# Eight expert weight tiles ahead instead of four, and the token rows written later

## The chip, the cores and the metric

The kernel runs on one core of one Trainium2 chip. The metric is the device time of one execution in microseconds (us). The engines are TensorE (PE; its weight loads are listed as PEld), VectorE (DVE), ScalarE (ACT), GpSimd (POOL) and SyncE (SP), which issues most of the DMA transfers. POOL issues the rest, among them the indirect ones, whose rows are picked by an index tile.

## The reference

256 tokens of width 1024 pass through two blocks, all in float32. The first has an HGRN/RG-LRU mixer, a convolutional feed-forward, an attention and a second feed-forward. The second has latent attention, a SwiGLU feed-forward, an S5 mixer, and at the end a mixture of experts. Only this last part is touched:

```
logits = t @ w_router                       # 256 tokens, 8 experts
top_vals, top_idx = lax.top_k(logits, 2)
gates = softmax(top_vals)
for e in range(8):                          # d_ff of an expert: 3584
    he  = (silu(t @ w_gate[e]) * (t @ w_up[e])) @ w_down[e]
    out = out + combine[:, e] * he
```

The reference runs every token through every expert and weighs by `combine`, which is zero but for a token's two experts. The kernel computes only the tokens that chose an expert.

## The kernel before

**Tiles of weights.** An expert has 28 tiles of 128 hidden columns, all eight have 224. A tile is 1.5 MB in float32: 1 MB for gate and up (`UP`), 0.5 MB for down (`DOWN`). They stream from memory once.

**Places in SBUF.** All weights ahead of the experts go through four slots of 3 MB, in turn, as 57 units (`LOADED`). The last four units are the second of the S5 input projection (slot 1) and the three of the S5 gated projection (`s5_glu`: slots 2, 3, 0). PE adds to `slot_free` when it is through with a unit (L1617): with `s5_glu` this is after output tiles 5, 11 and 15. The experts' ring of four tiles (`ups`, `downs`, L430 to L432) has three up parts in slot 1, and the fourth with the four down parts in slot 2. Slots 3 and 0 (`lone`, L434) hold the token rows: `hrow` (normalized tokens to be scattered), `xl` (rows of the next expert, read back) and `returned` (results read back).

**SP's order.** After the last unit SP waits for slots 1 and 2, loads tiles 0 to 3 into the ring (L490 to L496), and waits until PE has done the up part of tile 0 (L498). From then on it reloads the up part of a place as soon as PE's up part of the tile there is done (`up_ready`, L502), and the down part when PE's down part is (`moe_free`, L504).

**Gathering.** If no expert has over 96 tokens (`CAP`), which holds here, PE takes the `experts_gathered` path. It gathers the tokens of experts 0 and 1 from SBUF by two sets of matmuls (`gather`, L1772). The tokens of the later experts go through memory. DVE writes `hrow` (L2683). POOL waits for it and for the row numbers (`rows`, L549), scatters the rows into `rows_in` by four indirect DMAs (L551), and loads the rows of expert 2 into `xl` (`load`, L546). Expert 2's rows are needed by `turn_rows` at the end of expert 0. Rows of further experts follow, one load an expert, and each expert's result is stored (L561). At the last expert four indirect DMAs read results back (L564).

**PE's order.** `up(j)` is 64 weight loads and 64 matmuls as the trace counts them, `down(j)` 32 and 32. `four(e, i)` (L1846) is four tiles: up of tile j+1, then down of tile j. The program has it written out four times: in a loop of seven inside the loop over experts 0 to 5, in a loop of seven for expert 6, in a loop of six for expert 7, and once for the last four tiles. Between experts come `turn_rows`, `open_sums`, `turn_sums`. ACT (silu, L960) and DVE (`hidden`, L2647) work on each tile in between.

If an expert has over 96 tokens, a dense path runs in place of this (`experts_dense`); it did not run in the profiled execution.

Of the kernel before, what the change touches and what calls it, by code (L numbers as in the profile page):

```python
# [168 lines left out]
def build_program(nc, a):  # L169

    ctx = ExitStack()
    with ctx:
# [226 lines left out]
        gain_row = yT[:, 0:4].rearrange("p a n -> p (a n)")  # L399
        xg = part(12, 3).rearrange("p (a n) -> p a n", a=KD)  # L400
        first_picks = [part(i)[:, 0:2 * CAP].rearrange("p (g n) -> p g n", g=2) for i in (22, 23)]
        ye = part(18, 4)[0:CAP]
        weighted = part(17)[:, 0:2 * CAP].rearrange("p (g n) -> p g n", g=2)
        place = part(23)[0:CAP]
        ysum = part(26, 3).rearrange("p (a n) -> p a n", a=KD)
        posm = part(24)[:, 0:2 * 8].rearrange("p (g n) -> p g n", g=2)
# [22 lines left out]

        ring_slots = [(len(LOADED) - SLOTS + k) % SLOTS for k in range(2)]  # L430
        ups = [slots[ring_slots[h // 3]][:, h % 3 * UP:(h % 3 + 1) * UP] for h in range(RING)]
        downs = [slots[ring_slots[1]][:, UP + h * DOWN:UP + (h + 1) * DOWN] for h in range(RING)]  # L432

        lone = [slots[(len(LOADED) - SLOTS + k) % SLOTS] for k in (2, 3)]  # L434
        hrow = lone[0][:, 0:2 * D].rearrange("p (g d) -> p g d", g=2)
        xl = lone[0][0:CAP, 2 * D:3 * D]
        returned = lone[1][:, 0:4 * D].rearrange("p (n d) -> p n d", n=4)
        where = part(25)[:, 16:64].rearrange("p (n c) -> p n c", c=8)
# [7 lines left out]
        def _(sp):  # L446
# [8 lines left out]
            for name in STREAM:  # L455
                sizes, u0, w = phase_units(name), UNIT0[name], a["w_" + name]

                def load(u, unit, name=name, sizes=sizes, w=w, u0=u0):

                    sp.wait_ge(slot_free, unit + u0 + 1)  # L460
                    sp.dma_start(slots[(u0 + u) % SLOTS][:, 0:sizes[u]],
                                 w[bass.ds(unit, 1), :, 0:sizes[u]].rearrange("o p n -> p (o n)")
                                 ).then_inc(slot_loaded[(u0 + u) % SLOTS], 16)

                fours = len(sizes) // SLOTS if name in FFN and name != "ffn2" else 0
                if fours:
                    with sp.Fori(0, fours) as i:
                        for u in range(SLOTS):
                            load(u, i * SLOTS + u)
                for u in range(fours * SLOTS, len(sizes)):  # L470
                    if name == "even_in" and u == 0:
                        continue
                    load(u, u)
                    if name == "ffn2" and u == SLOTS - 1:
                        sp.wait_ge(x_ready, 6 * KD)
                        sp.dma_start(cT, a["s5_cT"]).then_inc(s5_loaded, 16)
                        sp.dma_start(bexp, a["s5_b"]).then_inc(s5_loaded, 16)
                    if name == "even_in" and u == 1:
                        for dst, small in ((rgw[:, :, :, :], "rgw"), (wf[:, :, :], "wf"),
                                           (wr[:, :, :], "wr"), (pos_i[:, :], "positions")):  # L480
                            sp.dma_start(dst, a[small]).then_inc(late_loaded, 16)
            def load_up(h, unit):
                sp.dma_start(ups[h], a["w_moe"][bass.ds(unit, 1), :, 0:UP].rearrange(
                                 "o p n -> p (o n)")).then_inc(moe_up_loaded[h], 16)
# [4 lines left out]

            for h in range(RING):  # L490
                for s in ring_slots[0:1 if h < 3 else 2]:
                    sp.wait_ge(slot_free, SLOTS + max(n for n in range(len(LOADED))
                                                      if n % SLOTS == s) + 1)
                load_up(h, h)
            for h in range(RING):
                load_down(h, h)  # L496
            last = EXPERTS * FE_TILES // RING - 1
            sp.wait_ge(up_ready, 2 * FT0["moe"] + 2)  # L498
            load_up(0, RING)
            with sp.Fori(1, last) as i:  # L500
                for h in range(RING):
                    sp.wait_ge(up_ready, i * (2 * RING) + (2 * (FT0["moe"] + h - RING) + 4))  # L502
                    load_up((h + 1) % RING, i * RING + (h + 1))
                    sp.wait_ge(moe_free, i * RING + h + 1)  # L504
                    load_down(h, i * RING + h)
# [15 lines left out]
        def _(pool):  # L521
# [26 lines left out]
            pool.wait_ge(mo["scattered"], ZEROED)  # L548
            pool.wait_ge(mo["rows"], 3)  # L549
            for n in range(4):  # L550
                pool.indirect_dma_start(  # L551
                    out=rows_in, out_offset=bass.IndirectOffsetOnAxis(ap=slot_row[:, n:n + 1], axis=0),
                    in_=hrow[:, n // 2], in_offset=None).then_inc(mo["scattered"], 16)
# [505 lines left out]
        def _(pe):  # L1059
# [643 lines left out]

            def up_weights(f, rounds):

                pe.wait_ge(moe_up_loaded[f % RING], rounds * 16 + 16 * (f // RING + 1))
                return ups[f % RING]

            def down_weights(f, rounds):

                pe.wait_ge(moe_down_loaded[f % RING], rounds * 16 + 16 * (f // RING + 1))
                return downs[f % RING]

            def experts_dense():
# [20 lines left out]
                for b in range(4):  # L1735
                    pe.matmul(ps[:, b, 0:1], ident, mask[:, 0:1], start=True, stop=False,
                              skip_group_check=True)
                with pe.Fori(0, EXPERTS) as e:
                    def up(f):
                        w = up_weights(f, e * (FE_TILES // RING))  # L1740
                        for k in range(2):
# [6 lines left out]
                    def down(f):  # L1748
                        w = down_weights(f, e * (FE_TILES // RING))
                        pe.wait_ge(hid_ready, e * FE_TILES + (FT0["moe"] + f + 1))  # L1750
# [6 lines left out]
                    for f in range(FE_TILES):  # L1757
                        if f + 1 < FE_TILES:
                            up(f + 1)
                        down(f)  # L1760
                pe.wait_ge(moe_free, RING + EXPERTS * FE_TILES)
                pe.sem_inc(acc_ready, KD)
# [7 lines left out]
            def experts_gathered():  # L1770
# [49 lines left out]
                def up(j, loads, inputs=None):  # L1820

                    pe.wait_ge(moe_up_loaded[j], loads)
                    for k in range(2):
                        for c in range(KD):
                            if inputs is not None and k == 0 and c % 4 == 0:
                                pe.wait_ge(mo["xready"], inputs + c // 4)
                            for s in range(0, P, STRIP):
                                o = (k * KD + c) * P + s
                                m = pe.matmul(gate_up(j, k)[s:s + STRIP],  # L1829
                                              ups[j][:, o:o + STRIP], xg[:, c], start=c == 0,  # L1830
                                              stop=c == KD - 1, skip_group_check=True)
                        m.then_inc(up_ready, 1)

                def down(j, loads, hids):

                    pe.wait_ge(moe_down_loaded[j], loads)
                    pe.wait_ge(hid_ready, hids)
                    for d in range(KD):
                        for s in range(0, P, STRIP):
                            o = d * P + s  # L1840
                            m = pe.matmul(y_sum(d)[s:s + STRIP], downs[j][:, o:o + STRIP],  # L1841
                                          hid[j][:, 0:CAP], start=False, stop=False,
                                          skip_group_check=True)
                    m.then_inc(moe_free, 1)

                def four(e, i, last=False):  # L1846

                    def at(scale, plus):
                        return e * (GROUPS * scale) + i * scale + plus

                    for j in range(RING):
                        if j < RING - 1:
                            up(j + 1, at(16, 16))
                        elif not last:
                            up(0, at(16, 32), at(2, 3))
                        down(j, at(16, 16), at(RING, FT0["moe"] + j + 1))

# [9 lines left out]
                gather(1)  # L1867
                up(0, 16, 1)
                open_sums(None)
                with pe.Fori(0, EXPERTS - 2) as e:  # L1870
                    with pe.Fori(0, GROUPS) as i:
# [70 lines left out]
        def _(dve):  # L1942
# [685 lines left out]
            def experts_gathered():  # L2628
# [52 lines left out]
                dve.wait_ge(mo["htaken"], 4)  # L2681
                for g in range(2):
                    dve.tensor_scalar(hrow[:, g], vtok[:, g], col[:, 2 + g:3 + g], None, ALU.mult  # L2683
                                      ).then_inc(mo["rows"], 1)
                for e in range(EXPERTS):
                    for f in range(FE_TILES):
# [4 lines left out]
                        if f == FE_TILES - 1 and e < EXPERTS - 1:  # L2691
                            dve.wait_ge(up_ready, 2 * (e * FE_TILES + FT0["moe"] + f) + 2)
                            take_input(e + 1)
                        hidden(e, f)
                        if e and f == 0:
                            take_turned(e - 1)
# [14 lines left out]
            def experts():  # L2711
                with dve.If(dve.value_load(crowded[0:1, 0:1], min_val=0, max_val=1) == 1):
                    dve.sem_inc(mo["rows"], 2)
                    dve.sem_inc(mo["yeready"], 2 * EXPERTS)
                    for g in range(2):
                        dve.tensor_scalar(mixd[g], ident, col[:, 2 + g:3 + g], None, ALU.mult
# [207 lines left out]
```

## Time and profile before

| | |
|---|---|
| median of 3 runs (lowest, highest) | 2221.22 us (2219.17, 2222.02) |
| profiled execution, span | 2221.2 us |
| profiled execution, own time | 2221.22 us, the same as its span |
| PE busy, DVE busy, ACT busy, POOL busy | 97%, 38%, 21%, 1% |
| the experts' first matmul on weights | 1291.91 us |
| weights of the experts | 224 tiles, 1 MB and 0.5 MB each |

All times of rows are counted from the start of the span. A busy PE is not PE at its peak, since the ends of matmuls are modelled; the rate is better read from the starts of like groups. PEld rows give where the weight loads stood still. "<-issue" at a row's end is idle time for which the profile shows no releaser. In the list of DMA queues q1 is SP's, q0 is POOL's, and q8 carries instructions.

### The profile page before, as it was taken

To read this page: it belongs to the slowest core of one execution; us is meant where nothing else is said; L and a number is where in the kernel's file an instruction comes from. 1 tells how busy PE (TensorE), PEld (TensorE's weight loads), DVE (VectorE), ACT (ScalarE), POOL (GpSimd) and SP (SyncE) were. 2 spreads that over 40 slices of the span, in tenths; PEclk is the share of its full clock that TensorE was granted. 3 is DMA by queue.
4 is the path that set the end of the run, shared out by engine and by line. 5 is a ranking of instruction groups with operands and counts; after the bars stand their busy time and mean duration, and the time that the engine had idled before them with its cause. 6 is when DMAs were issued, how large, how long until landed. Compare 5 with 4: busy or idle time off the path is not lost.

```text
span 2221.2 us, 67406 instructions
## 1 busy us (share of the span) xinstructions
PE 2161.3 (97%) x30418; PEld 2003.8 (90%) x30418; DVE 839.7 (38%) x2085; ACT 467.8 (21%) x1074; POOL 24.9 (1%) x43
## 2 busy tenths in 40 slices
PE   9999999999999999999987999999999999999998
PEld 8889999857999986999966889999999999999998
DVE  4257666224766636567769120101010101010102
ACT  3432112123211234110043121111111111111112
POOL 1000000000000000000000000000000000000000
PEclk9999999999999999999999999999999999999999
DMA  9242344232144322444322169999999999999996
GB/s 393 91 171 86 152 161 190 95 132 111 68 164 171 138 90 100 159 164 171 133 115 96 58 258 400 392 394 392 396 392 397 389 398 389 398 382 399 390 409 249
DMA packets 78400, 535.04 MB, mean 241 GB/s; under 512 B 8913, under 2 KB 9042, under 8 KB 41938
## 3 DMA queue, kind: packets, MB, share of 16 engines
q1 hardware_dynamic: 74450, 519.82, 59.6%
q0 software_dynamic: 3840, 13.63, 1.7%
q8 instruction: 83, 1.36, 0.3%
q14 instruction: 27, 0.22, 0.0%
HBM read 523.20 MB, written 10.22 MB: 240 GB/s over the span
## 4 chain that ended last, share of the span: by engine, by line
PE 69%; DVE 3%; ACT 1%; issue 1%; DVEq 0%; ACTq 0%
PE ps L1829 27%; PE ps L1841 13%; PE ps L1202 11%; PE ps L1244 7%; PE ps L1119 4%; PE ps L1611 2%; PE ps L1594 1%; DVE scr L2501 0%; PE ps L1793 0%; PE ps L1802 0%; PE ps L1135 0%; PE ps L1481 0%; PE ps L1467 0%; PE ps L1548 0%; PE ps L1443 0%
## 5 line engine op out<-in xcount | busy, mean ns | idle before, releaser
L1829 PE MATMUL ps<-scr,slot 128*64 128x96 f32 x14336 | 640.2, 246 | 3.2 <-issue 3.2
L1829 PEld LDWEIGHTS ps<-scr,slot 128*64 128x64 f32 x14336 | 613.0, 137 | 6.7 <-issue 6.6
L2650 DVE TENSOR_TENSOR scr<-scr,ps 128x96 f32<-128x96 f32 x224 | 56.8, 254 | 767.0 <-ACT scr L960 767.0
L1841 PE MATMUL ps<-scr,slot 128*64 128x96 f32 x7168 | 341.6, 246 | 1.3 <-issue 1.3
L1841 PEld LDWEIGHTS ps<-scr,slot 128*64 128x64 f32 x7168 | 317.0, 137 | 1.5 <-issue 1.5
L1244 PE MATMUL ps<-scr,slot 128*128 128x256 f32 x1056 | 237.6, 379 | 1.6 <-DVE scr L2321 1.6
L960 ACT ACTIVATE scr<-ps 128x96 f32<-128x96 f32 x224 | 56.3, 251 | 786.4 <-PE ps L1829 786.4
L1244 PEld LDWEIGHTS ps<-scr,slot 128*128 128x128 f32 x1056 | 196.2, 190 | 26.4 <-DVE scr L2321 2.0
L1202 PE MATMUL ps<-vtok,slot 128*128 128x128 f32 x1056 | 139.5, 275 | 0.0
L1202 PEld LDWEIGHTS ps<-vtok,slot 128*128 128x128 f32 x1056 | 128.8, 192 | 0.2
L1202 PE MATMUL ps<-vtok,proj 128*128 128x128 f32 x1056 | 128.7, 275 | 0.0
L1202 PEld LDWEIGHTS ps<-vtok,proj 128*128 128x128 f32 x1056 | 123.2, 192 | 0.0
L1202 PEld LDWEIGHTS ps<-hT,slot 128*128 128x128 f32 x960 | 116.2, 192 | 2.8
L1202 PE MATMUL ps<-hT,slot 128*128 128x128 f32 x960 | 116.9, 275 | 0.0
L1119 PE MATMUL ps<-hT,slot 128*128 128x256 f32 x416 | 94.1, 384 | 0.6 <-PE ps L1119 0.6
L2247 DVE TENSOR_TENSOR proj<-slot 128x512 f32<-128x512 f32 x132 | 91.1, 690 | 6.2 <-ACT mixT L724 2.9
L817 ACT ACTIVATE sq<-ps 128x128 f32<-128x128 f32 x66 | 18.3, 278 | 351.4 <-PE ps L1202 351.4
L1119 PEld LDWEIGHTS ps<-hT,slot 128*128 128x128 f32 x416 | 79.1, 192 | 13.7 <-issue 3.1
L1298 PE MATMUL ps<-hT,slot 128*128 128x256 f32 x384 | 88.3, 389 | 2.0 <-DMA slot<-in_w_even_in 1.7
L1298 PEld LDWEIGHTS ps<-hT,slot 128*128 128x128 f32 x384 | 74.6, 196 | 13.9 <-DMA slot<-in_w_even_in 1.9
L1119 PE MATMUL ps<-mixT,slot 128*128 128x256 f32 x384 | 84.6, 381 | 1.3 <-PE ps L1119 0.9
L1119 PEld LDWEIGHTS ps<-mixT,slot 128*128 128x128 f32 x384 | 72.4, 190 | 13.1 <-issue 3.0
(412 smaller groups left out, 2044.8 us busy)
## 6 DMA issues: line engine op xcount, KB each, us to landing
slot<-in_w_moe SPq DMA_DIRECT2D x224, 1024.0 KB, 7.0
slot<-in_w_moe SPq DMA_DIRECT2D x224, 512.0 KB, 6.9
slot<-in_w_ffn SPq DMA_DIRECT2D x33, 3072.0 KB, 10.7
slot<-in_w_even_in SPq DMA_DIRECT2D x3, 3072.0 KB, 27.5
slot<-in_w_odd_qk SPq DMA_DIRECT2D x2, 3072.0 KB, 10.5
slot<-in_w_s_glu SPq DMA_DIRECT2D x2, 3072.0 KB, 11.8
slot<-in_w_odd_v SPq DMA_DIRECT2D x2, 2048.0 KB, 8.1
slot<-in_w_even_in SPq DMA_DIRECT2D x2, 1536.0 KB, 10.6
```

What stands on the lines that cost most here:

```text
L817: act.activation(mid(k, 0), product(k, P1), ACT.Copy).then_inc(first_copied, 1)
L960: act.activation(gbuf[j][:, 0:CAP], gate_up(j, 0), ACT.Silu).then_inc(gate_act, 1)
L1119: m = pe.matmul(ps[:, bank0 + n % ring, 0:T], w[:, o:o + P], src[:, c], start=c == 0, stop=c == k - 1, skip_group_check=True)
L1202: m = pe.matmul(product(k, n), weights[:, c * P:(c + 1) * P], x[:, c], start=first and c == 0, stop=c == 3, skip_group_check=True)
L1244: m = pe.matmul(acc(d), w[:, o:o + P], hid2[u % 2][:, half], start=u == half == 0 and d % 2 == 0, stop=last, skip_group_check=True)
L1298: m = pe.matmul(even_tile(i), project.w[:, o:o + P], hT[:, c], start=c == 0, stop=c == KD - 1, skip_group_check=True)
L1594: m = pe.matmul(ps[k:k + 32, q % 2, a:b], w[:, r, q, k:k + 32], x[:, j, 0:n], start=False, stop=i == 3, skip_group_check=True)
L1611: m = pe.matmul(glu_tile(i), w[:, o:o + P], hT[:, c], start=c == 0, stop=c == KD - 1, skip_group_check=True)
L1829: m = pe.matmul(gate_up(j, k)[s:s + STRIP], ups[j][:, o:o + STRIP], xg[:, c], start=c == 0, stop=c == KD - 1, skip_group_check=True)
L1841: m = pe.matmul(y_sum(d)[s:s + STRIP], downs[j][:, o:o + STRIP], hid[j][:, 0:CAP], start=False, stop=False, skip_group_check=True)
L2247: dve.tensor_tensor(dst, a, b, ALU.subtract).then_inc(combined, 1)
L2650: dve.tensor_tensor(hid[f % 4][:, 0:CAP], gbuf[f % 4][:, 0:CAP], gate_up(f, 1), ALU.mult).then_inc(hid_ready, 1)
```

## The change

The ring of four moves from slots 1 and 2 to slots 3 and 0. Tiles 0 to 3 of the first expert get places of their own in slots 1 and 2 (`lead_ups`, `lead_downs`), with the same layout; the ring begins with tile 4. `hrow`, `xl` and `returned` move from slots 3 and 0 to slots 1 and 2, over the lead tiles, so DVE and POOL now wait until the lead tiles are used up (`moe_free` 8: four down parts done; its count starts at four). DVE writes the two halves of `hrow` after `hidden` of tiles 4 and 5 of expert 0. SP loads the lead tiles, then the ring as slots 3 and 0 come free, and waits for the up part of tile 4 before it reloads. PE writes the first four tiles out on their own, then has a loop of six for the rest of expert 0, then the loop over experts 1 to 5. The dense path, the narrowing of two tiles to their used columns, and a count added to `dve_own` in the dense path go with it.

```diff
-        ring_slots = [(len(LOADED) - SLOTS + k) % SLOTS for k in range(2)]
-        lone = [slots[(len(LOADED) - SLOTS + k) % SLOTS] for k in (2, 3)]
-        hrow = lone[0][:, 0:2 * D].rearrange("p (g d) -> p g d", g=2)
+        lead_slots, ring_slots = ([(len(LOADED) - SLOTS + k) % SLOTS for k in some]
+                                  for some in ((0, 1), (2, 3)))
+        lead_loaded = [_n[k] + 16 * n for k, n in zip(lead_slots, (3, 1 + RING))]
+        lead_ups, lead_downs = up_places(lead_slots), down_places(lead_slots)
+        ups, downs = up_places(ring_slots), down_places(ring_slots)
+        lead = [slots[k] for k in lead_slots]
+        hrow = lead[0][:, 0:2 * D].rearrange("p (g d) -> p g d", g=2)
...
             for h in range(RING):
+                for s in lead_slots[0:1 if h < 3 else 2]:
+                    sp.wait_ge(slot_free, left(s))
+                sp.dma_start(lead_ups[h], a["w_moe"][h, :, 0:UP]
+                             ).then_inc(slot_loaded[lead_slots[h // 3]], 16)
+            for h in range(RING):
+                sp.dma_start(lead_downs[h], a["w_moe"][h, :, UP:UP + DOWN]
+                             ).then_inc(slot_loaded[lead_slots[1]], 16)
+            for h in range(RING):
                 for s in ring_slots[0:1 if h < 3 else 2]:
-                load_up(h, h)
+                    sp.wait_ge(slot_free, left(s))
+                load_up(h, RING + h)
             for h in range(RING):
-                load_down(h, h)
+                load_down(h, RING + h)
-            sp.wait_ge(up_ready, 2 * FT0["moe"] + 2)
-            load_up(0, RING)
-            with sp.Fori(1, last) as i:
+            sp.wait_ge(up_ready, 2 * (FT0["moe"] + RING) + 2)
+            load_up(0, 2 * RING)
+            with sp.Fori(2, last) as i:
...
             pool.wait_ge(mo["rows"], 3)
+            pool.wait_ge(moe_free, RING + RING)
...
-                up(0, 16, 1)
+                up(0, None, 1)
                 open_sums(None)
-                with pe.Fori(0, EXPERTS - 2) as e:
+                four(0, 0, first=True)
+                with pe.Fori(1, GROUPS) as i:
+                    four(0, i)
+                turn_rows(16)
+                open_sums(2)
+                turn_sums(2)
+                with pe.Fori(1, EXPERTS - 2) as e:
...
-                for g in range(2):
-                    dve.tensor_scalar(hrow[:, g], vtok[:, g], col[:, 2 + g:3 + g], None, ALU.mult
-                                      ).then_inc(mo["rows"], 1)
...
                         hidden(e, f)
+                        if e == 0 and f in (RING, RING + 1):
+                            g = f - RING
+                            dve.wait_ge(moe_free, RING + RING)
+                            dve.tensor_scalar(hrow[:, g], vtok[:, g], col[:, 2 + g:3 + g], None,
+                                              ALU.mult).then_inc(mo["rows"], 1)
```

## Rows read from the trace of the kernel before

**Rows 1.** The page: busy time of PE; DMA share in 40 slices.

```profile
PE 2161.3 (97%) x30418; PEld 2003.8 (90%) x30418; DVE 839.7 (38%) x2085; ACT 467.8 (21%) x1074; POOL 24.9 (1%) x43
DMA  9242344232144322444322169999999999999996
```

**Rows 2.** Waits of PE and PEld, 1290 to 2221 us: total us, times, longest.

```profile
PE ps L1829 <- issue: 3.2, 10, 0.5
...
PEld ps L1829 <- issue: 6.6, 17, 1.2
```

**Rows 3.** Busy time by stretch: PE, PEld, DVE, ACT, POOL, clock, DMA, GB/s.

```profile
1320.00:1405.00 85.00, 85.00 (x2066) 85.00 (x2064) 5.34 (x21) 11.69 (x26) 0.00 (x0) 1.00 1.01 401
```

**Rows 4.** Timeline of PEld from the experts' start: start us, us, instructions.

```profile
1295.19 1.59 PEld L1829 LDWEIGHTS ps<-scr,slot 128*64 128x64 f32 x37
...
1299.83 0.44 PEld L1829 LDWEIGHTS ps<-scr,slot 128*64 128x64 f32 x9 [1.14 <-issue]
1300.15 1.44 PEld L1841 LDWEIGHTS ps<-scr,slot 128*64 128x64 f32 x32
1301.47 2.76 PEld L1829 LDWEIGHTS ps<-scr,slot 128*64 128x64 f32 x64
1304.11 1.44 PEld L1841 LDWEIGHTS ps<-scr,slot 128*64 128x64 f32 x32
...
1312.03 1.37 PEld L1841 LDWEIGHTS ps<-scr,slot 128*64 128x64 f32 x31
...
1315.47 2.82 PEld L1829 LDWEIGHTS ps<-scr,slot 128*64 128x64 f32 x63 [0.45 <-issue]
```

**Rows 5.** Timeline of POOL's DMA issues.

```profile
1294.19 1.04 POOL L551 DMA_INDIRECT rows_in<-slot,idx  x1 [1164.66 <-DVE slot L2683]
...
1298.09 0.96 POOL L551 DMA_INDIRECT rows_in<-slot,idx  x1 [0.30 <-issue]
1309.50 0.58 POOL L546 DMA_DIRECT2D slot<-rows_in  x1 [10.45 <-DMA rows_in<-slot,idx]
1412.83 0.53 POOL L546 DMA_DIRECT2D slot<-rows_in  x1 [102.75 <-PE ps L1793]
...
2102.80 1.01 POOL L564 DMA_INDIRECT slot<-rows_out,idx  x1 [4.51 <-DMA rows_out<-scr]
```

**Rows 6.** Timeline of PEld in the first passes for experts 6 and 7.

```profile
1986.71 2.70 PEld L1829 LDWEIGHTS ps<-scr,slot 128*64 128x64 f32 x64
...
1998.59 2.70 PEld L1829 LDWEIGHTS ps<-scr,slot 128*64 128x64 f32 x64
...
2104.35 0.30 PEld L1829 LDWEIGHTS ps<-scr,slot 128*64 128x64 f32 x5
...
2110.04 0.14 PEld L1841 LDWEIGHTS ps<-scr,slot 128*64 128x64 f32 x1
```

**Rows 7.** DMA queue q8, 1291 to 1317 us: packets, MB, share.

```profile
q8 instruction: 3, 0.05, 0.8%
```

**Rows 8.** The same queue, 1983 to 2004 us.

```profile
q8 instruction: 3, 0.05, 0.9%
```

**Rows 9.** SP's queue, 1301 to 1304 us.

```profile
q1 hardware_dynamic: 1, 0.00, 0.0%
```

**Rows 10.** L483, up parts from 1291 us on: issue to landing.

```profile
DMA to landing us min/median/max: 5.9/7.0/10.9
```

**Rows 11.** Timeline of SP's DMA issues around the experts' start.

```profile
1207.78 33.65 SPq L483 DMA_DIRECT2D slot<-in_w_moe  x4
...
1294.79 6.21 SPq L483 DMA_DIRECT2D slot<-in_w_moe  x2
```

**Rows 12.** Timeline of PEld behind `s5_glu` output tiles 11 and 15.

```profile
1264.26 0.20 PEld L1677 LDWEIGHTS ps<-cst,xT 128*128 128x128 f32 x2 [0.68 <-issue]
...
1279.75 0.20 PEld L1677 LDWEIGHTS ps<-cst,xT 128*128 128x128 f32 x2 [0.52 <-issue]
```

**Rows 13.** Timeline of DVE ahead of tile 0's hidden product.

```profile
1291.94 1.41 DVE L2683 TENSOR_SCALAR slot<-vtok,col 128x1024 f32<-128x1024 f32 x2
```

More of the change, by code:

```diff
@@ L399, in build_program @@
         gain_row = yT[:, 0:4].rearrange("p a n -> p (a n)")
-        xg = part(12, 3).rearrange("p (a n) -> p a n", a=KD)
+        xg = part(12, 3)[:, 0:KD * CAP].rearrange("p (a n) -> p a n", a=KD)
         first_picks = [part(i)[:, 0:2 * CAP].rearrange("p (g n) -> p g n", g=2) for i in (22, 23)]
@@ L404, in build_program @@
         place = part(23)[0:CAP]
-        ysum = part(26, 3).rearrange("p (a n) -> p a n", a=KD)
+        ysum = part(26, 3)[:, 0:KD * CAP].rearrange("p (a n) -> p a n", a=KD)
         posm = part(24)[:, 0:2 * 8].rearrange("p (g n) -> p g n", g=2)
@@ L428, in build_program, with up_places, down_places @@
         mix0 = {"even_out": 0, "odd_out": KD, "mla_o": 2 * KD}
-        ring_slots = [(len(LOADED) - SLOTS + k) % SLOTS for k in range(2)]
-        ups = [slots[ring_slots[h // 3]][:, h % 3 * UP:(h % 3 + 1) * UP] for h in range(RING)]
-        downs = [slots[ring_slots[1]][:, UP + h * DOWN:UP + (h + 1) * DOWN] for h in range(RING)]
-        lone = [slots[(len(LOADED) - SLOTS + k) % SLOTS] for k in (2, 3)]
-        hrow = lone[0][:, 0:2 * D].rearrange("p (g d) -> p g d", g=2)
-        xl = lone[0][0:CAP, 2 * D:3 * D]
-        returned = lone[1][:, 0:4 * D].rearrange("p (n d) -> p n d", n=4)
+        lead_slots, ring_slots = ([(len(LOADED) - SLOTS + k) % SLOTS for k in some]
+                                  for some in ((0, 1), (2, 3)))
+        def up_places(two):
+            return [slots[two[h // 3]][:, h % 3 * UP:(h % 3 + 1) * UP] for h in range(RING)]
+        def down_places(two):
+            return [slots[two[1]][:, UP + h * DOWN:UP + (h + 1) * DOWN] for h in range(RING)]
+        lead_loaded = [_n[k] + 16 * n for k, n in zip(lead_slots, (3, 1 + RING))]
[3 more added lines that the diff above has]
+        hrow = lead[0][:, 0:2 * D].rearrange("p (g d) -> p g d", g=2)
+        xl = lead[0][0:CAP, 2 * D:3 * D]
+        returned = lead[1][:, 0:4 * D].rearrange("p (n d) -> p n d", n=4)
         where = part(25)[:, 16:64].rearrange("p (n c) -> p n c", c=8)
@@ L481, in _, with left @@
                             sp.dma_start(dst, a[small]).then_inc(late_loaded, 16)
+            def left(s):
+                return SLOTS + max(n for n in range(len(LOADED)) if n % SLOTS == s) + 1
             def load_up(h, unit):
@@ L490, in _ @@
             for h in range(RING):
+                for s in lead_slots[0:1 if h < 3 else 2]:
[6 more added lines that the diff above has]
+            for h in range(RING):
                 for s in ring_slots[0:1 if h < 3 else 2]:
-                    sp.wait_ge(slot_free, SLOTS + max(n for n in range(len(LOADED))
-                                                      if n % SLOTS == s) + 1)
-                load_up(h, h)
+                    sp.wait_ge(slot_free, left(s))
+                load_up(h, RING + h)
             for h in range(RING):
-                load_down(h, h)
+                load_down(h, RING + h)
             last = EXPERTS * FE_TILES // RING - 1
-            sp.wait_ge(up_ready, 2 * FT0["moe"] + 2)
-            load_up(0, RING)
-            with sp.Fori(1, last) as i:
+            sp.wait_ge(up_ready, 2 * (FT0["moe"] + RING) + 2)
+            load_up(0, 2 * RING)
+            with sp.Fori(2, last) as i:
                 for h in range(RING):
@@ L1702, in router, with up_weights, down_weights @@
                           skip_group_check=True).then_inc(mo["pos"], 1)
-            def up_weights(f, rounds):
-                pe.wait_ge(moe_up_loaded[f % RING], rounds * 16 + 16 * (f // RING + 1))
-                return ups[f % RING]
-            def down_weights(f, rounds):
-                pe.wait_ge(moe_down_loaded[f % RING], rounds * 16 + 16 * (f // RING + 1))
+            def up_weights(e, f, first):
+                if first and f < RING:
+                    pe.wait_ge(slot_loaded[lead_slots[f // 3]], lead_loaded[f // 3])
+                    return lead_ups[f]
+                pe.wait_ge(moe_up_loaded[f % RING], e * (16 * GROUPS) + 16 * (f // RING))
+                return ups[f % RING]
+            def down_weights(e, f, first):
+                if first and f < RING:
+                    pe.wait_ge(slot_loaded[lead_slots[1]], lead_loaded[1])
+                    return lead_downs[f]
+                pe.wait_ge(moe_down_loaded[f % RING], e * (16 * GROUPS) + 16 * (f // RING))
                 return downs[f % RING]
@@ L1737, in experts_dense, with expert @@
                               skip_group_check=True)
-                with pe.Fori(0, EXPERTS) as e:
+                def expert(e, first):
                     def up(f):
-                        w = up_weights(f, e * (FE_TILES // RING))
+                        w = up_weights(e, f, first)
                         for k in range(2):
@@ L1748, in down @@
                     def down(f):
-                        w = down_weights(f, e * (FE_TILES // RING))
+                        w = down_weights(e, f, first)
                         pe.wait_ge(hid_ready, e * FE_TILES + (FT0["moe"] + f + 1))
@@ L1760, in experts_dense @@
                         down(f)
+                expert(0, True)
+                with pe.Fori(1, EXPERTS) as e:
+                    expert(e, False)
                 pe.wait_ge(moe_free, RING + EXPERTS * FE_TILES)
@@ L1820, in up @@
                 def up(j, loads, inputs=None):
-                    pe.wait_ge(moe_up_loaded[j], loads)
+                    if loads is None:
+                        pe.wait_ge(slot_loaded[lead_slots[j // 3]], lead_loaded[j // 3])
+                    else:
+                        pe.wait_ge(moe_up_loaded[j], loads)
+                    w = lead_ups[j] if loads is None else ups[j]
                     for k in range(2):
@@ L1829, in up @@
                                 m = pe.matmul(gate_up(j, k)[s:s + STRIP],
-                                              ups[j][:, o:o + STRIP], xg[:, c], start=c == 0,
+                                              w[:, o:o + STRIP], xg[:, c], start=c == 0,
                                               stop=c == KD - 1, skip_group_check=True)
@@ L1834, in down @@
                 def down(j, loads, hids):
-                    pe.wait_ge(moe_down_loaded[j], loads)
+                    if loads is None:
+                        pe.wait_ge(slot_loaded[lead_slots[1]], lead_loaded[1])
+                    else:
+                        pe.wait_ge(moe_down_loaded[j], loads)
+                    w = lead_downs[j] if loads is None else downs[j]
                     pe.wait_ge(hid_ready, hids)
@@ L1840, in down @@
                             o = d * P + s
-                            m = pe.matmul(y_sum(d)[s:s + STRIP], downs[j][:, o:o + STRIP],
+                            m = pe.matmul(y_sum(d)[s:s + STRIP], w[:, o:o + STRIP],
                                           hid[j][:, 0:CAP], start=False, stop=False,
@@ L1844, in down, with four @@
                     m.then_inc(moe_free, 1)
-                def four(e, i, last=False):
+                def four(e, i, last=False, first=False):
                     def at(scale, plus):
                         return e * (GROUPS * scale) + i * scale + plus
+                    here = None if first else at(16, 0)
                     for j in range(RING):
                         if j < RING - 1:
-                            up(j + 1, at(16, 16))
+                            up(j + 1, here)
                         elif not last:
-                            up(0, at(16, 32), at(2, 3))
-                        down(j, at(16, 16), at(RING, FT0["moe"] + j + 1))
+                            up(0, at(16, 16), at(2, 3))
+                        down(j, here, at(RING, FT0["moe"] + j + 1))
                 def open_sums(copies):
@@ L2714, in experts @@
                     dve.sem_inc(mo["yeready"], 2 * EXPERTS)
+                    dve.sem_inc(dve_own, 4)
                     for g in range(2):
```

## The prediction

> **What bounds the kernel now.** I read the page first, then the waits of PE, the stretches, the timelines of PE's weight loads, of POOL and of SP, and last the DMA queues. The page has PE busy for 97% of the span and the DMA engines at nine tenths from about 1290 us on [rows 1], so both could bound the experts. The stretches leave that open too: from 1320 to 1405 us PE shows no gap and DMA a share of 1.01 at 401 GB/s [rows 3]. Three rows decide it. No wait of PE behind 1290 us has a DMA as its releaser; what there is stands as "issue" [rows 2]. A tile takes 3.96 us, from one group of down loads at 1300.15 to the next at 1304.11, of which the up part is 2.64 and the down part 1.32 [rows 4]. A place of the ring is used again four tiles later, so its up part may take 15.84 - 2.64 = 13.2 us from issue to landing; the median is 7.0 and the longest 10.9 [rows 10]. PE sets the pace, weights come in time, and the 224 tiles cost 224 x 3.96 = 887 us whatever is loaded ahead.
>
> So the change can win only where PE stands still at the experts' beginning, and that is in two places. Up of tile 1 begins at 1295.19, and its down loads follow at 1300.15, 4.96 us later where 2.64 is usual: 2.32 us lost. A down part begins at 1312.03 and the next up part at 1315.47, 3.44 us for 1.32: 2.12 us lost [rows 4]. Together 4.4 us. Neither is a wait for weights: both stops fall inside a part, between loads from one tile that is already there. The queue that carries instructions moved three packets between 1291 and 1317 us [rows 7], while PE goes through its loop for the first time, so I read both stops as PE running out of instructions. That reading has a condition. Three packets were moved from 1983 to 2004 us too, as PE first went through expert 6's loop [rows 8], and the ups there keep their pace: from 1986.71 to 1998.59 are 11.88 us for three tiles, 3.96 each [rows 6]. What differs is POOL. Its four scatters are issued from 1294.19 to 1298.09, around the first stop, the load of expert 2's rows at 1309.50, just ahead of the second, and the four gathers of the results from 2102.80 [rows 5], around a third stop: an up part that begins at 2104.35 and reaches its down loads at 2110.04, 5.69 us for 2.64, 3.05 lost [rows 6]. So: new code costs 2 to 3 us where POOL's scatters, gathers or row loads are under way, and nothing beside weights and one plain store.
>
> **The change part by part.**
>
> *Loads ahead.* The lead tiles take the same places at the same times as tiles 0 to 3 now, from 1207.78 us on [rows 11]. New are the ring's first four tiles: 3 MB after `s5_glu` tile 11, at about 1264.3, and 3 MB after tile 15, at about 1279.8 [rows 12]. At 400 GB/s [rows 3] each takes 7.9 us (an estimate), so both have landed at about 1290, with DMA empty there before. The start of PE at 1295.19 hangs on the router's small steps, which touch no DMA: cost 0. If that cover fails it is one packet of code fetched beside 3 MB of weights, from 0 [rows 8] to 3.05 us [rows 6].
>
> *SP.* Its first reload now waits for the up part of tile 4: 1295.19 + 3 x 3.96 + 2.64 = 1309.7 us, against 1294.79 now [rows 11]. Behind that wait stand only later reloads, each with its 13.2 us as before. The stream ends no earlier and no later for PE: 0.
>
> *First four tiles.* They become straight code. From 1295.19 to 1311.0 us neither weights nor POOL move anything. I take the stop of 2.32 us as gone; the ends are 0 and 2.32 kept.
>
> *Token rows.* DVE loses two writes of 1.41 us together ahead of tile 0's hidden product [rows 13]; nobody waited for DVE there, so 0. They come back after tiles 4 and 5. The first waits for four down parts, at 1311.0; what is queued behind it is `hidden` of tile 5, not due before up of tile 5 ends at 1313.7, and the write takes half of 1.41. The second follows that product. Both are covered: 0. POOL's scatter then starts at about 1315 us (21 us later), and expert 2's rows are loaded 1309.50 - 1294.19 = 15.3 us behind it [rows 5], at about 1330; they are needed near 1410, so 0 by themselves.
>
> *Loop of six.* A new piece of code, entered at 1311.0 and through its first pass at 1326.9. The scatter falls into the middle of it, 4 us after entry; the gathers of expert 7 fell 6 us into a like pass and cost 3.05. I take the mean of the two measured scatter or gather stops, (2.32 + 3.05) / 2 = 2.7 us; the ends are 0 and 2.32 + 2.12 = 4.4. The load at 1330 comes when the pass is over, so I count no second stop.
>
> *Loop of experts 1 to 5.* One more piece that PE enters new, near 1412, as POOL loads rows at 1412.83 [rows 5] and stores a result. Expert 6's pass had the store alone and no stop [rows 6]. I take 0; the ends are 0 and 4.4.
>
> *Late weights.* The longest landing, 10.9 us, was reached with PE stopped for 4.4 us meanwhile, and with SP's queue getting nothing through from 1301 to 1304 [rows 9]. Without any stop it could be 10.9 + 4.4 = 15.3, 2.1 us over the 13.2. A stop of 2.7 in the same place gives that time back, so the two don't add: 0 beside it.
>
> Sum: -2.32 - 2.12 + 2.7 = -1.7 us. The profiled execution's own time is its span, 2221.2, which is also the median; so 2219.5.
>
> **A rule against it.** The two stops and a like pass without one are what the rows show [rows 4, 6]. The Trainium skill's page "Runtime: NRT & Kernel Launch", section "Instruction fetch mechanics", says that fetching runs ahead in sequence only, and that a taken branch whose target is outside a small window of pages stalls until the target is fetched. By that rule each new loop would pay at its back jump; the second stop does stand at the end of a first pass, but later passes of the same loop keep 3.96 a tile, which speaks against it as a general price. What it would make of this kernel is the third rival below.
>
> **The rivals.**
>
> 1. *No stop left.* The quiet four tiles also bring the code of the loop in time, and the scatter meets none that is new: -4.4, 2216.8. For: expert 6's pass. Against: all three passes with POOL's transfers had a stop.
> 2. *More code, more stops* (the other side). POOL's plain loads and stores are enough to hold up new code. Then both new loops have two stops: 2.7 + 2.12 in the loop of six and 2.32 + 2.12 in the next, 9.2 in place of 4.4, so +4.8, 2226.0. It decides from the entry into the loop of experts 1 to 5: a stop there makes it. For: the second stop came beside a plain load. Against: expert 6 with a store.
> 3. *The back jump.* Each new loop's first end costs 2.12: 2.7 + 2 x 2.12 = 6.9 against 4.4, so +2.5, 2223.7. For: where the second stop stands. Against: expert 7's loop shows none at its end.
> 4. *The stream is the bound after all.* Four tiles more ahead would then be worth 4 x 3.96 = 15.8 us: 2205.4. For: a DMA share of 1.01. Against: landings of 7.0 us for 13.2, and no wait of PE for a DMA. Here the change would do what its loads suggest; in all other cases they are simply not needed.
> 5. *The weights come late or the early loads disturb the router*: the stop at the first four or at 1290 stays or is replaced, +2.1 to +3.05 on the forecast, 2221.6 to 2222.6.
>
> **How the numbers follow.** Forecast 0.38, rival 1 0.17, rival 2 0.16, rival 3 0.12, rival 4 0.05, rival 5 0.12. A measurement of this kernel can tell about 0.2%, 4.4 us, from no change. Rival 4 and a good half of rival 1 are faster than that: 0.17. Most of rival 2 and a little of rivals 3 and 5 are slower: 0.17. The rest, 0.66, is the same within 0.2%. The range leaves out rival 4 and a few cases where stops add up: 2214 to 2227.5. The forecast's own range is 2217 to 2222.
>
> **What would show it.** Right: SP's loads at about 1264 and 1280 us; the tiles from 1295 to 1311 at 3.96 each; scatters from 1315; one stop of 2 to 3 us between 1315 and 1327; the entry near 1412 at full pace; no wait of PE for a DMA. Wrong: a stop before 1311 with nothing moving (then POOL is not the cause); a stop behind 1412; a wait for weights; a later start than 1295; or a tile that takes other than 3.96 us.

## The result: 3 us slower, and the profile after

The changed kernel takes 2222.43 us (median of 20 runs, 2218.90 to 2228.82), the kernel before 2219.51 us in 20 runs beside it (2217.65 to 2222.97). The ratio is 1.0014, 95% interval 1.0008 to 1.0021, so the change costs about 3.1 us (1.8 to 4.7). I had forecast 1.7 us less. The profiled execution of the changed kernel took 2219.58 us and its span is 2217.5 us: what lies around a span is about 2 us (1.8 to 2.4 in the other profiles below that list both). The profile of before that I worked from, with a span of 2221.2, therefore belongs to an execution of some 2223.3 us (an estimate), almost 4 above the median. My step "the profiled execution's own time is its span, 2221.2, which is also the median" was wrong, and so is the line of the table of times above that says the same. Two executions, of 4534 us (before, beside e5 to e8) and 5309 us (e8), took more than twice the usual time and are left out of all medians and ratios.

The page of the changed kernel: the queue that carries instructions moved 89 packets, where it moved 83 before (the line by itself), six more for the code that is written out.

```profile
span 2217.5 us, 67375 instructions
...
q8 instruction: 89, 1.46, 0.3%
```

```profile
q8 instruction: 83, 1.36, 0.3%
```

PEld's timeline from the experts' start, the counterpart of [rows 4]:

```profile
1294.97 2.67 PEld L1866 LDWEIGHTS ps<-scr,slot 128*64 128x64 f32 x64
...
1310.78 2.70 PEld L1866 LDWEIGHTS ps<-scr,slot 128*64 128x64 f32 x64
1313.42 1.38 PEld L1882 LDWEIGHTS ps<-scr,slot 128*64 128x64 f32 x32
1314.74 1.38 PEld L1866 LDWEIGHTS ps<-scr,slot 128*64 128x64 f32 x32
1316.50 1.35 PEld L1866 LDWEIGHTS ps<-scr,slot 128*64 128x64 f32 x32 [0.38 <-issue]
1317.80 1.38 PEld L1882 LDWEIGHTS ps<-scr,slot 128*64 128x64 f32 x32
1319.12 2.70 PEld L1866 LDWEIGHTS ps<-scr,slot 128*64 128x64 f32 x64
1323.37 1.36 PEld L1882 LDWEIGHTS ps<-scr,slot 128*64 128x64 f32 x32 [1.55 <-issue]
...
1329.81 2.91 PEld L1866 LDWEIGHTS ps<-scr,slot 128*64 128x64 f32 x64 [0.32 <-issue]
```

The four written-out tiles run from 1294.97 to 1310.78: 15.8 us, their full pace. The first pass through the loop of six runs from there to 1329.81: 19.0 us for 15.84, so 3.2 lost. Read in the same way, the first pass of before lost 4.4 [rows 4].

SP's and POOL's issues, the counterparts of [rows 11] and [rows 5]:

```profile
1262.23 16.02 SPq L497 DMA_DIRECT2D slot<-in_w_moe  x4
1278.29 2.35 SPq L501 DMA_DIRECT2D slot<-in_w_moe  x4
1309.75 4.47 SPq L497 DMA_DIRECT2D slot<-in_w_moe  x2
```

```profile
1315.75 1.04 POOL L573 DMA_INDIRECT rows_in<-slot,idx  x1 [1186.23 <-PE ps L1882]
...
1319.65 0.96 POOL L573 DMA_INDIRECT rows_in<-slot,idx  x1 [0.30 <-issue]
1334.07 0.58 POOL L567 DMA_DIRECT2D slot<-rows_in  x1 [13.46 <-DMA rows_in<-slot,idx]
```

The up parts of the ring from issue to landing, for [rows 10]; a place allows 13.2 us:

```profile
DMA to landing us min/median/max: 4.9/7.0/12.3
```

And stretches, with the columns of [rows 3]: the gathers, the four lead tiles, and behind the scatter.

```profile
1284.00:1292.00 8.00, 7.29 (x136) 7.30 (x138) 4.51 (x22) 2.27 (x3) 0.00 (x0) 0.79 0.41 167
1295.00:1311.00 16.00, 16.00 (x389) 16.00 (x390) 1.09 (x5) 2.29 (x5) 0.00 (x0) 1.00 0.06 9
...
1335.00:1405.00 70.00, 70.00 (x1702) 70.00 (x1700) 5.09 (x19) 10.09 (x23) 0.00 (x0) 1.00 1.02 412
```

### The profile page after: what moved, and what is told of

It is laid out like the page before. It is cut to its first block, busy times and chain, and to the rows that moved or that the text cites. A ratio compares the mean times of both kernels' runs of the same rounds, so it can differ in the third digit from the quotient of the medians.

```text
span 2217.5 us, 67375 instructions
## 1 busy us (share of the span) xinstructions
PE 2161.5 (97%) x30418; PEld 2005.8 (90%) x30418; DVE 840.0 (38%) x2085; ACT 467.7 (21%) x1074; POOL 24.8 (1%) x43
## 4 chain that ended last, share of the span: by engine, by line
PE 69%; DVE 3%; ACT 1%; issue 1%; DVEq 0%; ACTq 0%
PE ps L1866 27%; PE ps L1882 13%; PE ps L1224 11%; PE ps L1266 7%; PE ps L1141 4%; PE ps L1633 2%; PE ps L1616 1%; DVE scr L2549 0%; PE ps L1826 0%; PE ps L1835 0%; PE ps L1813 0%; PE ps L1157 0%; PE ps L1503 0%; PE ps L1489 0%; PE ps L1570 0%
```

## Experiments

All are compared below in one view: what PEld waited for "issue" between 1295 and 2204 us, that is inside the experts (total us, times, longest). Some 1.3 us of it is the usual 0.18 at each turn from one expert to the next, as e7 shows. For the profile of before that row is in [rows 2]; the down parts' row, here, makes it 8.1 us.

```profile
PEld ps L1841 <- issue: 1.5, 1, 1.5
```

| kernel | issue waits, us | median, us | ratio to before, 95% interval |
|---|---|---|---|
| before, profile read ahead | 8.1 | 2219.51 | |
| b_look1, b_look2 (before again) | 2.9, 2.4 | 2219.27, 2225.66 (one run each) | |
| after; a_look1 (after again) | 5.0; 6.3 | 2222.43; 2220.23 (one run) | 1.0014 (1.0008 to 1.0021) |
| e1_code_only | 5.9 | 2223.73 | 1.0016 (1.0007 to 1.0024) |
| e2_late_rows | 1.7, and 2.3 for weights | 2219.93 | 0.9999 (0.9990 to 1.0007) |
| e3_rows_early | 4.8 | 2222.10 | 1.0003 (0.9992 to 1.0014) |
| e4_ring_held | 7.7 | 2224.61 | 1.0024 (1.0015 to 1.0033) |
| e5_rows_spaced | 1.5 | 2219.12 | 1.0002 (0.9993 to 1.0011) |
| e6_second_loop_only; e6_look1 | 3.8; 4.9 | 2221.34; 2220.29 (one run) | 1.0014 (1.0005 to 1.0023) |
| e7_quarter_before | 1.3 | 2217.73 | 0.9994 (0.9986 to 1.0003) |
| e8_quarter_code | 1.3 | 2217.30 | 0.9989 (0.9980 to 0.9998) |

The runs of before beside e1 to e4 have a median of 2219.22 us, those beside e5 to e8 2219.19.

**e1_code_only.** PE's code split as in the change, all else as before.

```diff
                 open_sums(None)
-                with pe.Fori(0, EXPERTS - 2) as e:
+                four(0, 0)
+                with pe.Fori(1, GROUPS) as i:
+                    four(0, i)
+                turn_rows(16)
+                open_sums(2)
+                turn_sums(2)
+                with pe.Fori(1, EXPERTS - 2) as e:
```

> The kernel before, with one part of the change: PE's first four tiles written out on their own, a loop of six for the rest of expert 0, then the loop over experts 1 to 5. Places, loads and token rows stay as before. Code theory (PE stands still for 1 to 3 us where it enters code for the first time while POOL moves rows): two more passes are entered new, so 2 to 5 us slower than before, with stops in the trace near 1297, near 1315 and perhaps behind 1412. Early-load theory (the ring's 6 MB ahead of the experts disturb the S5 tail and the gathers) and late-weight theory (the late scatter delays reloads past the 13.2 us they have): no change, within 1 us of before.

Measured: +3.5 us by the ratio (1.6 to 5.3), as much as the whole change. PEld's waits in e1, and the stops in the loop of six:

```profile
PEld ps L1829 <- issue: 3.7, 10, 1.1
PEld ps L1841 <- issue: 2.2, 3, 1.0
```

```profile
1312.15 2.67 PEld L1829 LDWEIGHTS ps<-scr,slot 128*64 128x64 f32 x63 [1.12 <-issue]
...
1318.47 1.35 PEld L1829 LDWEIGHTS ps<-scr,slot 128*64 128x64 f32 x32 [1.01 <-issue]
...
1324.79 1.36 PEld L1841 LDWEIGHTS ps<-scr,slot 128*64 128x64 f32 x32 [1.01 <-issue]
...
1330.99 0.20 PEld L1841 LDWEIGHTS ps<-scr,slot 128*64 128x64 f32 x3 [0.98 <-issue]
```

The split alone is enough; neither the early loads nor the late rows are needed for the loss. The place differs from what I expected: nothing stops near 1297, though new code, weights and the scatter (issued from 1294.10 to 1298.00) meet there. The four stops of 1.0 to 1.1 us stand in the loop of six.

**e2_late_rows.** The kernel before with the change's waits and order on POOL and DVE (`pool.wait_ge(moe_free, RING + RING)`, `hrow` written after tiles 4 and 5).

> The kernel before, with another part alone: the token rows are written after tiles 4 and 5 and scattered after four tiles are used up; PE's code and all weight loads stay as before. Code theory: the scatter now meets a loop that PE has been through once, and the first pass has weights alone beside it, so the two stops of the first pass (4.4 us in the profile of before) go, and the kernel is 1.5 to 4 us faster than before. Late-weight theory: scatter and reloads run beside a PE that does not stop, up parts land later than 13 us and PE waits for a DMA: 1 to 3 us slower. Early-load theory: no change.

Measured: no change. The stops in the code nearly go, and a wait for weights takes their place:

```profile
PEld ps L1830 <- DMA slot<-in_w_moe: 2.3, 2, 1.5
PEld ps L1830 <- issue: 1.7, 9, 0.3
```

Up parts issued from 1330 to 1340 us, issue to landing:

```profile
DMA to landing us min/median/max: 13.9/14.1/14.3
```

That is over the 13.2 us of a place. In the profile both theories had a half of it. The time, between 2.2 us faster and 1.6 slower, shows neither.

**e3_rows_early.** The changed kernel, `hrow` in `hT`, written and scattered at once; `load(2)` alone waits for the lead tiles.

```diff
-        hrow = lead[0][:, 0:2 * D].rearrange("p (g d) -> p g d", g=2)
+        hrow = hT[:].rearrange("p a n -> p (a n)").rearrange("p (g d) -> p g d", g=2)
...
             pool.wait_ge(mo["rows"], 3)
-            pool.wait_ge(moe_free, RING + RING)
...
             pool.wait_ge(mo["scattered"], ZEROED + 16 * 4)
+            pool.wait_ge(moe_free, RING + RING)
             load(2)
```

> The changed kernel, but the token rows are written and scattered as early as before, out of a tile that is free by then (hT); only the load of expert 2's rows waits for the lead tiles. The scatter then runs beside the four tiles that need no weights, and the loop of six has only weights and one row load beside it. Late-weight theory: no wait is left, time of before (0 to 1 us). Code theory: the written-out tiles may stop once (2.3 us) and the loop of six no longer does at the scatter, so about the changed kernel or 1 to 2 us better, +1 to +3 against before. Early-load theory: +3 as in the changed kernel.

Measured: 1.0003, with an interval that holds both no change and the whole loss of the change, so the time decides nothing. Its profile has 4.8 us of issue waits, 1.8 of them in three stops in the first pass of the loop of six (ending at 1321.24, 1327.01 and 1332.62 us). The scatter was issued long before, from 1295.69 to 1299.59, but the load of expert 2's rows only at 1315.70, so this run does not show that weights alone make a stop. e4 and e6 do.

**e4_ring_held.** The changed kernel, with `sp.wait_ge(mo["gathered"], 4)` ahead of the ring's first eight loads.

> The changed kernel, but SP holds the ring's first eight loads (tiles 4 to 7) until PE has done both gathers, at about 1291 us; they run beside the four lead tiles. Early-load theory: the S5 tail and the gathers are as before, so the time of before (0 to 1 us). Code theory and late-weight theory: about +3 us against before, as in the changed kernel; the written-out four tiles keep 3.96 us each, since they have weights alone beside them.

Measured: +5.3 us (3.3 to 7.3), against 3.1 for the change. Without the early loads the loss stays, and is if anything larger, so these loads are not its cause. The lead tiles now have weights beside them and do not all keep the full pace that I had expected: one stop of 0.44 us ends at 1306.22, where POOL's queue moves nothing (its first scatter is issued at 1316.41). So weights alone are enough for a stop; POOL's rows are not needed, which my reading ahead of the result had made them. In all, the issue waits are the longest of all profiles but the one read ahead:

```profile
PEld ps L1883 <- issue: 5.4, 5, 2.4
PEld ps L1867 <- issue: 2.3, 10, 0.5
```

**e5_rows_spaced.** The kernel before, with one more line in POOL's loop over the four scatters: `pool.wait_ge(moe_free, RING + (n + 1) * RING)`.

> The kernel before, with the four scatters spread out: the first waits for four used tiles, each next one for four more (about 16 us apart); PE's code, all places, DVE's writes and the weight loads stay as before. Transfer-debt theory (weights need 397 GB/s of some 410 to 420; what POOL moves beside them has to be paid by landings that come later, and a landing that comes later holds up either the next piece of PE's code or the next weights): the first pass has weights alone and each scatter adds 1.3 us to the landings, which shrink again until the next; longest landing about 10 us, no stop over 0.5 us in the experts' first 60 us, 1 to 3 us faster than before. If stops come from new code whatever DMA does: no change, 0 to 1 us.

Measured: 1.0002. Up parts land after 5 to 10.2 us until 1360, as expected, and in the profile the stops are gone, as in the kernels with a quarter of the loads:

```profile
PEld ps L1830 <- issue: 1.5, 8, 0.3
```

The time does not show it: the forecast of 1 to 3 us less is outside all but the edge of the interval (1.6 us faster to 2.4 slower). There was less to win than I thought, see e7.

**e6_second_loop_only.** Of e1's split the second half alone: expert 0 as a loop of seven, then the loop over experts 1 to 5.

> The kernel before, with expert 0's loop of seven written out apart from the loop over experts 1 to 5: one more pass of new code, entered near 1412 us, when PE has looped for 100 us; the first four tiles aren't written out. Transfer-debt theory: landings are 7 us there, so this pass stops for 0.2 to 1 us in all, and the kernel is 0 to 1 us slower than before; the changed kernel's 3 us come from the first two passes behind one another. My rival 2 (each new loop pays the full stops): 2 to 4.4 us slower.

Measured: +3 us by the ratio (1.1 to 5.1), +2 by the medians. The expectation of 0 to 1 fails. But the pass behind 1412 us, the one that is added, has no stop in the two profiles. What both have more than b_look1 and b_look2 lies in the first passes for experts 6 and 7: 0.9 and 0.4 us (e6), 0.7 and 1.7 (e6_look1), against 0.2 and 0 (b_look1), 0 and 0.2 (b_look2). In expert 6's pass POOL has issued one plain store by then, at 1983.64 and at 1981.65 us. The added code moves all code behind it. Whether that is the cause was not tried.

**e7_quarter_before and e8_quarter_code.** The kernel before, and e1, with a quarter of each tile loaded:

```diff
-                sp.dma_start(ups[h], a["w_moe"][bass.ds(unit, 1), :, 0:UP].rearrange(
+                sp.dma_start(ups[h][:, 0:UP // 4], a["w_moe"][bass.ds(unit, 1), :, 0:UP // 4].rearrange(
...
-                sp.dma_start(downs[h], a["w_moe"][bass.ds(unit, 1), :, UP:UP + DOWN].rearrange(
+                sp.dma_start(downs[h][:, 0:DOWN // 4], a["w_moe"][bass.ds(unit, 1), :, UP:UP + DOWN // 4].rearrange(
```

> The kernel before, with a quarter of each expert tile loaded (the first columns of its up and its down part; PE multiplies by what else lies there), so weights ask for about 100 GB/s. PE's work and code are the same. Transfer-debt theory: PE finds its code and weights always in time, no stop over 0.3 us behind 1292 us, 3 to 5 us faster than before. If stops come from new code whatever DMA does: time of before, stops as before.

> The kernel with PE's code split as in the change (e1), and a quarter of each expert tile loaded as in e7. Transfer-debt theory: the split costs nothing here, within 1 us of e7. If new code costs by itself: 3 to 4 us above e7, as the split costs with full loads.

PEld's waits in e7, then in e8:

```profile
PEld ps L1829 <- issue: 1.3, 7, 0.2
```

```profile
PEld ps L1829 <- issue: 1.3, 7, 0.2
```

Up parts from issue to landing in e8, from 1320 us on:

```profile
DMA to landing us min/median/max: 2.5/2.7/6.0
```

The split that costs 3.5 us beside full loads costs nothing beside a quarter of them (2217.30 against 2217.73 us). So PE stands still where it enters new code beside a full stream of weights, and not because of the code as such.

That it is the code that comes late is shown by the queue of instructions. In e1 a packet of 16 KB starts between 1322.2 and 1322.3 us. It takes 1.10 us (68.7% of what 16 engines have in 0.1 us), and the stop that stands there ends at 1324.79, 1.4 us after the packet has landed:

```profile
q8 instruction: 1, 0.02, 68.7%
```

In both profiles of the changed kernel, in e1 and in e4, all 18 issue waits of over 0.35 us inside the experts end 1.2 to 1.5 us after such a landing. The split adds two passes of four tiles and six packets, so one packet is work for 15.84 / 3 = 5.3 us of PE (an estimate). The four packets of e1's stops start at 1309.85, 1315.97, 1322.26 and 1328.45 us, 6.1 to 6.3 apart, so each comes some 0.9 us later than PE needs it. In e8 six packets start from 1299.53 to 1325.72, 5.2 apart on the mean. The counts, first in e1 from 1309 to 1329 us, then in e8 from 1299 to 1326:

```profile
q8 instruction: 4, 0.07, 1.3%
```

```profile
q8 instruction: 6, 0.10, 1.3%
```

With no stop at all the kernel before is 1.5 us faster by the medians (interval: 3.1 faster to 0.7 slower), where I had expected 3 to 5: its stops cost less than the 4.4 us that I set out to win back.

**Second profiles.** Kernels of before, after and e6, unchanged, for one execution each.

> The kernel before once more, for a second profile. If the profile that I forecast from was an unlucky one (its stops inside the experts' tiles sum to 8.0 us, 4.4 of them in the first pass): first-pass stops of 0 to 2.5 us, all stops 1 to 4 us, the stretch from the first up part to the last down part about 908.4 (its length with a quarter of the loads) + 1 to 4 us. If it was typical: 8 us again, about 916.

> The same kernel for a third profile: as for b_look1, and by the unlucky-profile reading another sum of stops than in the second, by 1 us or more.

> The changed kernel for a second profile. Written-out four tiles without a stop again; stops of 2.5 to 5 us in the first pass through the loop of six; 0.2 to 1 us behind 1412; all stops 4 to 7 us.

> The kernel with the second loop alone (e6) for a second profile, since its first shows no stop behind 1412 where the added pass is and yet it was timed 2 to 3 us above before. Transfer-debt theory: stops of 0 to 1 us behind 1412 again. Rival (a pass of new code pays anywhere): 1 to 3 us there in this execution.

PEld's waits in b_look1:

```profile
PEld ps L1829 <- issue: 1.7, 8, 0.5
PEld ps L1841 <- issue: 1.2, 2, 1.0
```

In b_look2:

```profile
PEld ps L1829 <- issue: 1.9, 9, 0.5
...
PEld ps L1841 <- issue: 0.5, 1, 0.5
```

In the changed kernel, a_look1:

```profile
PEld ps L1882 <- issue: 3.7, 3, 1.8
PEld ps L1866 <- issue: 2.6, 10, 0.7
```

The mean of after's two profiles less that of b_look1 and b_look2 is 5.65 - 2.65 = 3.0 us, and 3.1 were measured. The first profile of before, with 8.1, was far from its fellows. Leaving it out is a choice made with the result known: with it before's mean is 4.5 and the difference 1.2 us. (b_look2 is the slowest of these runs for a reason ahead of the experts: its first up part starts at 1300.5 us, that of b_look1 at 1293.4.) The first pass, from tile 1's up part to the next pass, takes 17.0 us in b_look2:

```profile
1303.90 2.67 PEld L1829 LDWEIGHTS ps<-scr,slot 128*64 128x64 f32 x64
...
1320.86 2.82 PEld L1829 LDWEIGHTS ps<-scr,slot 128*64 128x64 f32 x63 [0.46 <-issue]
```

That is 1.1 us over 15.84; in b_look1 it is 1.9 and in the profile read ahead 4.4.

No version that loads all its weights is measurably faster than the kernel before. e5 removes the stops from its profile, but all that there is to win is about 1.5 us, 0.07%, by e7; e8, by its ratio, has 2.4 (0.4 to 4.4).

## Why the prediction was wrong, by its own steps

*What bounds the kernel.* Right: PE sets the pace. The tiles keep 3.96 us after the change, no wait of PE for a DMA appears, and with a quarter of the loads the kernel gains about 1.5 us, 3.1 at the end of the interval. Rival 4 (the stream is the bound) is out.

*"So the change can win only where PE stands still ... Together 4.4 us."* Here the sum broke. The two stops are real, but their size came from one execution. In two more the first pass lost 1.9 and 1.1 us. The term -2.32 - 2.12 should have been about -1.5. Only the second stop is shown to be late code: it ends 1.4 us after a packet that lands at 1313.48, like the stops above. The first is made of four pauses that end from 1296.94 to 1299.83, while the queue of instructions moves nothing (from 1296.62 to 1305.60), beside POOL's scatters; the stop beside the gathers has such short pauses too. Neither b_look1 nor b_look2 has these pauses beside the same transfers, and what they were stays open.

*First four tiles: stop gone.* Right, in both profiles of the changed kernel. The lead tiles do give PE a quiet start.

*Loop of six: 2.7 us.* Mis-sized the other way: 3.2 us, and 3.8 in a_look1, in three stops, not one. With a typical first pass of 1.5 these two terms alone make +2.

*Loop of experts 1 to 5: 0.* 0.25 us in both profiles. Rival 2 put its weight here; it has the sign of the result but not its place.

*What the sum left out.* The passes for experts 6 and 7, whose code is not touched, but moves: 0.6 and 1.3 us in the pass for expert 7 after, 0 and 0.2 in b_look1 and b_look2 (the profile read ahead, with 3.05, is left out here too). Together: -1.5 + 3.5 + 0.25 + 0.8 = +3.0 us.

*"New code costs 2 to 3 us where POOL's scatters, gathers or row loads are under way, and nothing beside weights and one plain store."* Half right. e8 against e1 shows that the traffic makes the stop, e4 and e6 that it can be weights without POOL's scatters, gathers or row loads. Rival 3, with +2.5, came nearest to the measured 3.1, but by luck: the pause right at the first back jump of the loop of six is 0.32 us after the change, not 2.12, and in e8 PE takes the same back jumps and stops at none. By the rule of the Trainium skill's "Runtime: NRT & Kernel Launch", section "Instruction fetch mechanics", a jump out of a small window must fetch. The trace of e8 speaks against it for this loop: from 1327 to 1416 us PE takes five back jumps and the queue moves one packet. The same section of the Trainium skill says that fetching is hidden, because instructions are dispatched more slowly than they are filled in. e1 (5.9 us of waits) and e4 (7.7) show where it is not.

*Early loads: 0.* Right; without them e4 is no faster. The gathers of the profiled execution did lose 1.6 us (PEld from 1284.70 to 1291.60, 6.9 us where before has 5.25), for another reason: PE's clock was granted at half, 1.2 of 2.4 GHz, for 3.4 us from 1285.8 on, and the stretch shows a mean of 0.79. b_look2 has the same at 1294.3 with no early load, so it does not take the change; before stood idle as long at the router just ahead and kept its clock, so what decides it stays open.

*Late weights: 0 beside a stop.* Right as a mechanism: the longest landing is 12.3 of 13.2 us after the change, and e2, in which PE does not stop, goes over it and waits. *Times of the steps:* ring loads at 1262.2 and 1278.3 (1264 and 1280 expected), scatter at 1315.75 (1315), row load at 1334.1 (1330).

Still open: what moves e6's loss to experts 6 and 7, and why a pass directly behind other new code stops more often than one behind a loop. The packets suggest for the second that 6.2 us for each 5.3 us of work use up, pass by pass, what was fetched ahead; no run varied that.

## What to carry to other kernels

Loading further ahead won nothing here, where the ring already lands in half of its time; ask first which wait ends last. Writing a loop out a second time is not free: beside a saturated stream of weights each new pass of code can stop PE, and here that cost 3 us. A stop of a few us in one profile has to be seen in a second profile before a gain is computed from it, and a profile's span set against the spread of the timed runs first.

## What the runs showed of the hardware

A transfer of 2 MB beside a stream of weights that needs 397 GB/s (1.5 MB in 3.96 us), where the fullest stretch of the changed kernel shows 412, is felt for long: in e2 up parts land after 14.1 us at 1330 to 1340 and still after 9.2 at 1410 to 1430, where 7 is usual. In e2 PE pays for it with 2.3 us of waits for weights; spread out over 60 us (e5) PE pays nothing. And code is not fetched again while a loop runs, though three packets of 16 KB are moved as PE enters such a loop: between 1350 and 1416 us of the changed kernel the queue moved none.
